# Splitting a weight sum earlier and spreading the activation sums in a two-layer encoder's dense layers

## The reference, cut to what matters

```
def sqrelu_mlp(h, w1, w2):
    u = jax.nn.relu(jnp.einsum('bsd,df->bsf', h, w1))
    return jnp.einsum('bsf,fd->bsd', u * u, w2)
...
for i in range(2):
    hn = rmsnorm(h, norm_mix[i])
    mix = conformer_conv(hn, ...) if i == 0 else pool_mixer(hn, pool_w, pool_b, pool_scale)
    h = h + mix
    h = h + sqrelu_mlp(rmsnorm(h, norm_mlp[i]), mlp_w1[i], mlp_w2[i])
return rmsnorm(h, final_norm)
```

## Time and profile before

| | us |
|---|---|
| median of three runs | 920.83 |
| the profiled execution, its own time | 920.28 |
| its span, first to last instruction | 918.7 |
| TensorE busy | 879.2 |
| VectorE busy | 751.0 |
| ScalarE busy | 496.3 |
| GpSimd (POOL) busy | 197.7 |
| mean granted TensorE clock, share of full | 0.984 |

### The profile page before, as it was taken

One profiled execution on the slowest core, in us unless ns is written; L12 is line 12 of the kernel. 1 busy time (PEld: TensorE's weight loads), 2 busy tenths in 40 slices (PEclk: granted clock), 3 DMA queues, 4 the chain that ended last, 5 costly groups with the idle time before them and its releaser, 6 DMA issues.

```text
span 918.7 us, 13173 instructions
## 1 busy us (share of the span) xinstructions
PE 879.2 (96%) x4815; PEld 760.8 (83%) x4815; DVE 751.0 (82%) x938; ACT 496.3 (54%) x707; POOL 197.7 (22%) x168
## 2 busy tenths in 40 slices
PE   8999999998998998999898999899899989998997
PEld 8888887897878887988796889888698888888886
DVE  5899998869987958795888888897888678678976
ACT  6889885346363634546363654455374637354443
POOL 1699950731021011101102040001110110111000
PEclk9999999999999999999998999999999999999999
DMA  9775640334466664646584213236664556745402
GB/s 306 181 175 141 166 115 24 115 115 92 138 118 141 178 160 114 161 117 157 115 241 164 76 46 116 46 96 158 135 162 159 115 120 174 184 117 138 138 1 92
DMA packets 80435, 121.91 MB, mean 133 GB/s; under 512 B 3034, under 2 KB 41954, under 8 KB 79492
## 3 DMA queue, kind: packets, MB, share of 16 engines
q1 hardware_dynamic: 62116, 89.54, 29.2%
q0 software_dynamic: 18128, 31.46, 20.8%
q10 hardware_dynamic: 144, 0.26, 0.1%
HBM read 111.82 MB, written 2.10 MB: 124 GB/s over the span
## 4 chain that ended last, share of the span: by engine, by line
PE 58%; DVE 16%; DMA 8%; issue 6%; POOL 6%; ACT 4%; DVEq 0%; POOLq 0%; SPq 0%; ACTq 0%
PE ps L1798 8%; PE ps L1796 8%; PE ps L1797 8%; PE ps L2096 5%; PE ps L2097 5%; PE ps L2098 5%; PE ps L2062 4%; PE ps L2063 4%; PE ps L2064 4%; DMA w_raw<-in_mlp_w 4%; DMA b_sum<-in_mlp_w 3%; DVE w_lo L1467 2%; POOL merged_a L535 2%; POOL merged_b L535 2%; POOL w_lo L518 2%
## 5 line engine op out<-in xcount | busy, mean ns | idle before, releaser
L1796 PE MATMUL ps<-act_hi,w_hi 128*128 128x512 f32 (+1 forms) x496 | 180.2, 363 | 0.0
L1798 PE MATMUL ps<-act_hi,w_lo 128*128 128x512 f32 (+1 forms) x496 | 179.5, 362 | 0.0
L1797 PE MATMUL ps<-act_lo,w_hi 128*128 128x512 f32 (+1 forms) x496 | 179.5, 362 | 0.0
L2096 PE MATMUL ps<-w_hi,u_hi 128*128 128x512 f32 x392 | 156.7, 400 | 12.8 <-DVE u_lo L1462 12.8
L2098 PE MATMUL ps<-w_hi,u_lo 128*128 128x512 f32 x392 | 155.1, 396 | 0.0
L2097 PE MATMUL ps<-w_lo,u_hi 128*128 128x512 f32 x392 | 155.1, 396 | 0.0
L584 POOL DMA_DIRECT2D b_sum<-in_mlp_w x28 | 33.5, 1195 | 396.3 <-DVE w_lo L1467 396.3
L1798 PEld LDWEIGHTS ps<-act_hi,w_lo 128*128 128x128 f32 x496 | 93.6, 189 | 14.5
L1797 PEld LDWEIGHTS ps<-act_lo,w_hi 128*128 128x128 f32 x496 | 93.7, 189 | 14.4
L1796 PEld LDWEIGHTS ps<-act_hi,w_hi 128*128 128x128 f32 x496 | 93.6, 189 | 14.2
L2096 PEld LDWEIGHTS ps<-w_hi,u_hi 128*128 128x128 f32 x392 | 75.3, 192 | 31.5 <-DVE u_lo L1462 12.4
(11 more groups left out here) (285 smaller groups left out, 1941.1 us busy)
## 6 DMA issues: line engine op xcount, KB each, us to landing
w_raw<-in_mlp_w SPq DMA_DIRECT2D x66, 512.0 KB, 4.6
w_raw<-in_mlp_w SPq DMA_DIRECT2D x10, 2048.0 KB, 7.7
b_sum<-in_mlp_w POOLq DMA_DIRECT2D x28, 512.0 KB, 5.9
w_raw<-in_mlp_w POOLq DMA_DIRECT2D x18, 512.0 KB, 6.4
w_raw<-in_conv_w SPq DMA_DIRECT2D x16, 512.0 KB, 5.6
prod_a<-prod_a POOLq DMA_DIRECT2D x7, 1024.0 KB, 7.9
b_sum<-in_mlp_w SPq DMA_DIRECT2D x14, 512.0 KB, 3.4
w_raw<-in_conv_w SPq DMA_DIRECT2D x2, 2048.0 KB, 11.4
```

The costliest lines, as they stand in the source:

```text
L1796: nc.tensor.matmul(dst, lh, rh, start=(n == 0), stop=False)
L1797: nc.tensor.matmul(dst, lh, rl, start=False, stop=False)
L1798: return nc.tensor.matmul(dst, ll, rh, start=False, stop=(n == count - 1))
L2096: nc.tensor.matmul(dst, lh, rh, start=(f == 0 and (opens or i not in (0, 3))), stop=False)
```

## The change

It changes the place of some operations in the engines' lists and the way two of the activation sums get their operands:

1. In a plain group `early_part(1)` (ScalarE, high part of S1) moves ahead of the fourth quarter's `up_tile`, and `w_low(1)` (VectorE) to right behind `w_low(0)`, ahead of `b_low(3)`. `W_AT`, the order in which the seven weight parts are ready, is changed to match.
2. `w_sum_three` moves from ahead of `add(5)` to behind it.
3. In a first group ScalarE copies two activation blocks from the transposes' PSUM banks (`x_copy`, four copies), where VectorE added high and low parts; VectorE then makes one sum ahead of `third_sum` and two blocks behind `a_low(1)`. The other three sums and all four high and low parts move into the first plain group (`opens=True`), which is taken out of the loop.
4. SP's two pooling loads move behind both loads of the eighth group's w2.

```
@@ constants
-W_AT = (1, 3, 4, 2, 5, 7, 6)
+W_AT = (1, 2, 4, 3, 5, 7, 6)
-X_SUMS = 8
+X_SUMS = 6
+X_COPIES = 4
+X_AT = (2, 3, 1, 4)
@@ SP, load_groups
                 pair(PAIRS - 1, closes=True)
-                if layer == 0:
-                    sp.wait_ge(up_mm, block_part(0, PAIRS - 1) + PARTS)
-                    sp.dma_start(gain[:, 1, :], row(pool_scale[0])).then_inc(gain_in[1], 16)
-                    sp.dma_start(pw_raw, pool_w[0].rearrange("g (k p) d -> p (g k) d", p=P)).then_inc(pw_in, 16)
                 last = 7 * (MIDDLE - 1) + splits
                 sp.wait_ge(w2_lo_ok, last + 5)
                 load_m2(layer, GROUPS - 1, 0)
                 sp.wait_ge(w2_lo_ok, last + 7)
                 load_m2(layer, GROUPS - 1, 1)
+                if layer == 0:
+                    sp.wait_ge(up_mm, block_part(0, PAIRS - 1) + PARTS)
+                    sp.dma_start(gain[:, 1, :], row(pool_scale[0])).then_inc(gain_in[1], 16)
+                    sp.dma_start(pw_raw, pool_w[0].rearrange("g (k p) d -> p (g k) d", p=P)).then_inc(pw_in, 16)
@@ ScalarE
+            def x_copy(gen, b):
+                at = slice((b - 2) * P, (b - 1) * P)
+                act.wait_ge(act_lo_ok, 4 * gen + b + 1)
+                for into, half in ((z3, 0), (z1, 1)):
+                    nc.scalar.copy(into[:, :, at], turn_banks(gen, b)[:, 4 * half:4 * half + 4]).then_inc(x_copied, 1)
...
             w1_high(0, 0, 3)
+            x_copy(GEN_MLP0, 2)
             act_high(GEN_MLP0, 3)
...
             act_high(GEN_MLP1, 3)
+            x_copy(GEN_MLP1, 2)
...
+            def x_high(layer, k, summed):
+                act.wait_ge(x_sum_ok, X_SUMS * layer + summed)
+                nc.scalar.copy(x_hi[k], x_parts[k]).then_inc(x_hi_ok, 1)
@@ ScalarE, mlp_middle of a first or plain group
                         first_b()
+                        x_copy((GEN_MLP0, GEN_MLP1)[layer], 3)
                     first_sum_b()
...
                     a_high(1)
+                    if opens:
+                        x_high(layer, 2, 1)
+                        x_high(layer, 0, 5)
                     if kind == "plain":
                         early_part(layer, v, 0)
                     up_tile(n + 2, done + 3, banks[2], squared[1][:, 0], lambda: chain_b(3, 1))
+                    if opens:
+                        x_high(layer, 1, 4)
+                        x_high(layer, 3, 6)
+                    if kind == "plain":
+                        early_part(layer, v, 1)
                     up_tile(n + 3, done + 4, banks[3], squared[1][:, 1])
...
                 a_high(4)
-                if kind == "plain":
-                    early_part(layer, v, 1)
...
-                    x_high(0, 6)
-                    x_high(1, 6)
-                    x_high(2, 6)
-                    x_high(3, 8)
@@ VectorE, mlp_middle of a first or plain group
                     if kind == "first":
-                        dve.wait_ge(act_lo_ok, 4 * (GEN_MLP0, GEN_MLP1)[layer] + NB)
-                        x_block(layer, 1, z1, 1, 1)
-                        x_block(layer, 2, z3, 0, 1)
-                        x_step(layer, 3, z3, z1, z3, ALU.subtract)
-                        x_block(layer, 4, z2, 0, 0)
-                        x_step(layer, 5, z2, z3, z2, ALU.add)
-                        x_step(layer, 6, z1, z1, z2, ALU.subtract)
+                        dve.wait_ge(x_copied, X_COPIES * (layer + 1))
+                        x_step(layer, 1, z3, z1, z3, ALU.subtract)
+                    if opens:
+                        x_step(layer, 4, z2, z3, z2, ALU.add)
+                        x_step(layer, 5, z1, z1, z2, ALU.subtract)
+                        x_step(layer, 6, z4, z4, z2, ALU.subtract)
                     third_sum(n + 2)
                     a_low(0)
                     a_low(1)
+                    if kind == "first":
+                        x_block(layer, 2, z2, 0, 0)
+                        if layer:
+                            dve.wait_ge(pb_ok, 1)
+                        x_block(layer, 3, z4, 1, 0)
+                    if opens:
+                        x_low(layer, 2)
+                        x_low(layer, 0)
+                        x_low(layer, 1)
+                        x_low(layer, 3)
                     if kind == "plain":
                         w_low(layer, v, 0)
+                        w_low(layer, v, 1)
                     b_low(3)
...
                 a_low(4)
-                if kind == "plain":
-                    w_low(layer, v, 1)
...
                 if kind == "plain":
                     w_low(layer, v, 2)
-                    w_sum_three()
...
                 add(5, 6, h[:, 2:4, 0:512])
+                if kind == "plain":
+                    w_sum_three()
                 add(6, 8, h[:, 0:2, 512:D])
...
-                    x_low(layer, 0)
-                    if layer:
-                        dve.wait_ge(pb_ok, 1)
-                    x_block(layer, 7, z4, 1, 0)
-                    x_step(layer, 8, z4, z4, z2, ALU.subtract)
-                    x_low(layer, 1)
-                    x_low(layer, 2)
-                    x_low(layer, 3)
@@ ScalarE and VectorE, both layers
             mlp_middle(0, 0, "first")
-            with act.Fori(0, PAIRS) as v:
+            mlp_middle(0, 0, "plain", opens=True)
+            mlp_middle(0, 0, "blocks")
+            with act.Fori(1, PAIRS) as v:
```

More of the change, by code:

```diff
@@ L236, in hybrid_encoder @@
         b_chain_added, b_t3_ok, b_t1_ok = sem("b_chain_added"), sem("b_t3_ok"), sem("b_t1_ok")
-        x_sum_ok, x_hi_ok, x_lo_ok = sem("x_sum_ok"), sem("x_hi_ok"), sem("x_lo_ok")
+        x_copied, x_sum_ok, x_hi_ok, x_lo_ok = (sem(n) for n in ("x_copied", "x_sum_ok", "x_hi_ok", "x_lo_ok"))
         p1_copied, up_sum_ok, acc_out_ok = (sem(n) for n in ("p1_copied", "up_sum_ok", "acc_out_ok"))
@@ L903, in mlp_up_last, with mlp_middle @@
                         nc.scalar.copy(pw_hi[:], pw_raw).then_inc(pw_hi_ok, 1)
-            def mlp_middle(layer, v, kind):
+            def x_high(layer, k, summed):
+                act.wait_ge(x_sum_ok, X_SUMS * layer + summed)
+                nc.scalar.copy(x_hi[k], x_parts[k]).then_inc(x_hi_ok, 1)
+            def mlp_middle(layer, v, kind, opens=False):
                 w = {"first": 0, "plain": 2 * v + 1, "blocks": 2 * v + 2}[kind]
@@ L998, in mlp_middle @@
                 a_high(4)
-                if kind == "plain":
-                    early_part(layer, v, 1)
-                elif kind == "blocks":
+                if kind == "blocks":
                     next_w1(layer, v + 1, 0, block_part(layer, v) + PARTS)
                     next_w1(layer, v + 1, 1, block_part(layer, v) + PARTS)
-                else:
+                elif kind == "first":
                     next_w1(layer, 0, 0, done + GF)
@@ L1022, in mlp_middle @@
                     next_w1(layer, 0, 3, done + GF)
-                    def x_high(k, summed):
-                        act.wait_ge(x_sum_ok, X_SUMS * layer + summed)
-                        nc.scalar.copy(x_hi[k], x_parts[k]).then_inc(x_hi_ok, 1)
-                    x_high(0, 6)
-                    x_high(1, 6)
-                    x_high(2, 6)
-                    x_high(3, 8)
             mlp_middle(0, 0, "first")
-            with act.Fori(0, PAIRS) as v:
+            mlp_middle(0, 0, "plain", opens=True)
+            mlp_middle(0, 0, "blocks")
+            with act.Fori(1, PAIRS) as v:
                 mlp_middle(0, v, "plain")
@@ L1074, in _ @@
             act_high(GEN_MLP1, 3)
+            x_copy(GEN_MLP1, 2)
             mlp_middle(1, 0, "first")
-            with act.Fori(0, PAIRS) as v:
+            mlp_middle(1, 0, "plain", opens=True)
+            mlp_middle(1, 0, "blocks")
+            with act.Fori(1, PAIRS) as v:
                 mlp_middle(1, v, "plain")
@@ L1401, in x_low @@
             def x_low(layer, k):
-                dve.wait_ge(x_hi_ok, X_PARTS * layer + k + 1)
+                dve.wait_ge(x_hi_ok, X_PARTS * layer + X_AT[k])
                 if k == 1:
@@ L1652, in _ @@
             mlp_middle(0, 0, "first")
-            with dve.Fori(0, PAIRS) as v:
+            mlp_middle(0, 0, "plain", opens=True)
+            mlp_middle(0, 0, "blocks")
+            with dve.Fori(1, PAIRS) as v:
                 mlp_middle(0, v, "plain")
@@ L2054, in mlp_up_blocks @@
                     else:
-                        pe.wait_ge(x_lo_ok, X_PARTS * layer + right[i] + 1)
+                        pe.wait_ge(x_lo_ok, X_PARTS * layer + X_AT[right[i]])
                         rh, rl = x_hi[right[i]], x_lo[right[i]]
```

## The result

The changed kernel takes 882.42 us (median of 4 runs, 881.22 to 883.08), the kernel before, run beside it, 921.51 (4 runs, 919.5 to 922.97). The ratio is 0.9576, with a 95% interval of 0.9553 to 0.9598. The forecast was 884, in a range of 879 to 896. The profiled execution took 883.08 us, 37.2 less than the 920.28 of before, against 36.7 forecast.

What follows compares the result with a forecast made beforehand. TensorE's work, waits and lowered clock bound the kernel. Of 42.0 us recoverable, 2.1, 1.1, 1.7 and 0.4 stay, leaving 36.7; 920.28 becomes 883.6, plus 0.55 for the median: 884 us, range 879 to 896.

Steps and rivals of the forecast that it cites:

- What bounds it: TensorE, busy 96% of the span: waits 28.7, hidden idle 1.8 and clock 11.5, at most 42.0 us to recover.
- Parts 1 and 2: Ahead of blocks groups: S2 leaves earlier, all six waits for add(5) go, 15.9 + 1.0 us, 1.5 to spare.
- the first groups: Waits of 3.61 and 3.62 us go; T2 brings new ones of 1.1 and 1.7 at down product 1.
- First plain groups: Head of each layer's first plain group: 0.9 us waits return at down product 2; 2.1 us stay in total.
- Part 4: Layer 0's last blocks group: T4 lands without the pooling loads beside it, and the 3.75 us wait goes.
- The 0.4 us forecast for their new place: POOL's multiplies in the eighth group: VectorE loses 3.0 us against 3.1 of cover; cost nothing to 0.4, 0.4 taken.
- 2.70 is a delay of 1.5, not of 2.84: b_low(5) beside POOL's multiplies took 2.70 instead of 1.22 us; used against the multiplies rival's full block.
- multiplies shut VectorE out: Rival: POOL's multiplies block VectorE for their whole 5.7 us instead of 3.0; 888 us, chance 0.08.
- choking: Rival: added VectorE and ScalarE work chokes the first plain groups, with waits and clock falls; 894 us, chance 0.14.
- fall of the clock: Rival: TensorE's clock falls all the same without the long waits; 895.5 us, chance 0.05.
- The "slower" rival: Plain groups: S1's cast delays the fourth quarter's relu and down product 1; 921 us at 19 us flight, chance 0.03.

Runs made afterwards that it cites:

- e2: Changed kernel with S1's high and low part back behind a_high(4) and a_low(4), and w_sum_three back ahead of add(5); 905.07 us.
- after: The changed kernel, with all four parts of the change; 882.42 us.
- before: The kernel without the change; 921.51 us.
- e6: On e1, POOL's multiplies held until VectorE has made the last low part of this layer's w2 before the eighth group; 888.52 us.
- e1: Changed kernel with the two pooling loads back in their old place; 888.68 us.
- e3: Kernel before with parts 1, 2 and 4, activation sums still made in the first groups; 896.82 us.
- e9: On e3, S1's high part cast behind the fourth quarter's relu and square, its low part made behind fourth_sum; 891.21 us.
- e10: Changed kernel with S1's high part behind the fourth quarter's relu and square, its low part behind fourth_sum; 881.92 us.
- e4: Kernel before with only w_sum_three moved behind add(5); 909.9 us.

## Why the prediction was right, point by point

**What bounds it** held. TensorE's time is its work plus its waits plus the clock, and removing the waits gave the clock's share back with them. That the number came out within 0.5 us is in part luck: the forecast had 5.3 of the 42.0 left and 4.5 are, while the clock gave some 10.7 and not 11.5. Some of the terms below miss by more than their sum does.

**Parts 1 and 2** held in mechanism and size: no wait where 15.9 us stood, S2 out 17.4 ahead of the blocks group, 1.3 us to spare where 1.5 was forecast. By removal (e2) the two are worth 22.7 us, where 15.9 + 1.0 of waits and 4.5 of clock make 21.4. In e2's trace the six waits are 16.1 and TensorE is busy for 6.8 more than in after (874.5 and 867.7), since one of the four falls lasts 6.8 us. The landing was taken as 9.3 and measured 8.0.

**Part 3**, the first groups: 3.61 and 3.62 gone, a new wait at product 1 behind T2 and the fourth relu, forecast 1.1 and 1.7, measured 0.82 and 1.54. T2 took 7.4 and 7.1 us. **First plain groups**: the term was 2 × 0.9 at product 2, and that step was oversized: 0.29 each. `a_low(2)` was forecast to end at 266.4 for a product due at 265.5; in after it ends at about 262.6 (half of `261.83 1.43 DVE L1478`) for a product due at 262.3, so VectorE was 0.6 us quicker than worked out. (Some of that was a slip: 274.2 − 13.8 is 260.4, not 260.2, and the product was counted from 260.0, which is where it does start in before.) What it missed instead is the wait ahead of that group, 0.32 and 0.31 for `add(5)` of the first group, which nobody had looked at since the earlier trace rows has none there. The two errors nearly cancel: 1.2 + 0.6 against 1.8.

**Part 4**: 3.75 and its 2.7 of clock gone, as forecast; by removal 6.3 of 6.45, and `a_low(5)` has 1.9 to spare, as forecast (482.6 for 484.5). Both halves of the reason are needed, but the second was read too small. T4's late landing uses up those 1.9 and costs 0.25 itself (e6). The multiplies were taken to hold VectorE by 1.5 us, and hold it by 3.8, in `b_low(5)` and `a_low(5)` (e1). The 0.4 us forecast for their new place was 0: they land among adds that read PSUM.

**POOL and VectorE.** The forecast read "2.70 is a delay of 1.5, not of 2.84" as evidence against a full block. It was none. 2.84 is the mean of a multiply of 2.40 and one of 3.31, and an operation that comes during a multiply is delayed only by what is left of it. In e1 `b_low(5)` comes 1.74 us before the first multiply ends and is 1.61 longer than alone; `a_low(5)` comes 2.28 before the second ends and is 2.15 longer. The second multiply comes while `b_low(5)` is at work, and is 0.91 longer in its turn. The Trainium skill (SBUF — State Buffer, "Who interferes with whom") states that a VectorE operation with two SBUF inputs and a GpSimd one that reads SBUF share a port and the second is blocked fully; the runs agree with it (in e1 both delays are within 0.13 us of the rest of the multiply; in e6 two low parts take 5.59 beside 5.97 of multiplies). Its other half, that a VectorE operation with at most one SBUF input is left alone, agrees too: 1.27 and 1.28 for two adds from PSUM beside the multiplies, as without them. So the rival "multiplies shut VectorE out" was right as a mechanism and fell because of where the multiplies land.

**The rivals.** No choking and no fall of the clock. The "slower" rival, which had 0.03, is real as a mechanism: S1's cast in front of a relu made 2.47 and 2.57 us of waiting in e3. The forecast had weighed it in plain group v = 1, where S1 has 12 us; in v = 0 the kernel before has some 7, since there S1 leaves at the same 255 as in e3. What keeps it away in the changed kernel is part 3, by the 10.7 us above, which the forecast didn't see. Even so S1 took 9.7 us there, more than the 9.3 that the forecast took for the longest, and landed 1.5 before its cast began (255.54). It costs 5.6 us where the sums stay in the first groups (e3 less e9), not 36.

**How the parts add up.** Taken back one at a time, the three cost 6.3 (part 4), 22.7 (1 and 2) and 14.4 (3): 43.4, while all of them together are 39.1. The surplus is e3's side effect: part 3 is worth 14.4 with S1's cast ahead of the relu and 9.3 with it behind (e9 less e10), so 5.1 of the 14.4 belong to both.

## What to carry to other kernels

Where one engine is busy for 96% of the span, list its waits, and look at the granted clock right behind each: a wait of 2.5 to 4 us here often cost another 1.5 to 2.9. Moving a load's cast forward in a strictly ordered list is safe only as long as its DMA has landed; ask which product waits for whatever stands behind it, and try it behind that (e10 got the same time without the risk). When a wait is taken for one cause, hold that cause alone in a run and read the trace, not the time: e6 had the time that one theory gave and a trace that contradicts it.

## What the runs showed of the hardware

The clock fell to its lower level in stretches of 3.4 or 6.8 us behind waits of TensorE, and the length of the wait doesn't decide it alone. In a long wait it can fall before the wait is over, as in e1 at 472.2, in the wait that ends at 473.56. It fell behind 1.87 (e4), 2.57 and 2.65 (before), 2.61, 2.63 and 2.64 (e2), 2.47 and 2.57 (e3), and behind every one of 2.85 or more; it didn't behind 1.91 (e4), 2.50 and 2.52 (e2), 2.51, 2.56 and 2.74 (before), nor behind any of 1.54 or less. The forecast's "after waits of 2.57 to 3.75 only" was a limit that one kernel's few waits suggested; what else decides stays open. Nor is the cost fixed: behind the same wait (3.75 and 3.68) the lower level lasted 6.8 us before and 3.4 in e4. It varies between executions of one kernel as well: the fastest of the kernel before, 917.84 us, had a mean granted clock of 0.990, and one of 922.81 us had 0.980.

Two POOL multiplies of 2.40 us each stretched a VectorE subtraction of 1.22 and one of 0.68 to 2.83 each, or a pair of 2.35 to 5.59, and the second of them grew to 3.3. They left adds with one PSUM input at their 1.27 for two. Where an operation of POOL must lie beside VectorE's work, the adds from PSUM are the place for it.
